# Small parameters on ScalarE's queue, input tiles turned first, and pick counts summed on TensorE, in a fused attention, state-space, convolution and mixture-of-experts layer

## The reference

```
h    = rms_norm(x, mix_norm);  proj = h @ w_in
c_q, c_kv, k_pe, u_ssm, conv_a, conv_g = split(proj)
y    = [rms(attention(c_q, c_kv, k_pe)), rms(s5(u_ssm)), rms(conv(conv_a, conv_g))]
x    = x + y @ w_out
h    = rms_norm(x, ffn_norm)
group     = argmax(h @ w_grp + b_grp)                 # 4 groups
two picks = top 2 of softmax((h @ w_exp + b_exp)[group])   # 8 experts in a group
x    = x + sum over the 2 picks: gate * ((silu(h @ w1[e]) * (h @ w3[e])) @ w2[e])
```

## Time and profile before

| | us |
|---|---|
| median of three runs | 1185.1 |
| the profiled execution | 1186.63 |
| its span, from first to last instruction | 1184.9 |
| TensorE busy | 1123.3 (95%) |
| VectorE busy | 977.1 (82%) |
| ScalarE busy | 704.5 (59%) |
| POOL busy | 372.2 (31%) |
| mean granted TensorE clock | 0.988 |

### The profile page before, as it was taken

One profiled execution on the slowest core, in us unless ns is written; L12 is line 12 of the kernel. 1 busy time (PEld: TensorE's weight loads), 2 busy tenths in 40 slices (PEclk: granted clock), 3 DMA queues, 4 the chain that ended last, 5 costly groups with the idle time before them and its releaser, 6 DMA issues.

```text
span 1184.9 us, 16010 instructions
## 1 busy us (share of the span) xinstructions
PE 1123.3 (95%) x5762; PEld 870.5 (73%) x5762; DVE 977.1 (82%) x1203; ACT 704.5 (59%) x825; POOL 372.2 (31%) x350
## 2 busy tenths in 40 slices
PE   6999999889999799998899999999999999999996
PEld 3457464766676577888788888888888888888885
DVE  5999989666666754367999999999999999999993
ACT  6521226655465541223577777777777777777772
POOL 4231012378971000112223323323323333333321
PEclk9999999999999999998999999999999999999998
DMA  8300010000006012236999999999999999999962
GB/s 294 95 1 1 1 25 5 1 1 2 1 2 249 1 37 83 84 127 235 387 369 373 374 397 379 390 400 386 393 379 391 391 367 372 395 378 369 388 236 55
DMA packets 40840, 260.96 MB, mean 220 GB/s; under 512 B 16366, under 2 KB 17114, under 8 KB 26970
## 3 DMA queue, kind: packets, MB, share of 16 engines
q1 hardware_dynamic: 30698, 243.03, 52.1%
q0 software_dynamic: 10096, 17.34, 6.0%
HBM read 252.26 MB, written 26.35 MB: 235 GB/s over the span
## 4 chain that ended last, share of the span: by engine, by line
PE 83%; DVE 9%; ACT 3%; issue 2%; DMA 1%; POOL 0%; POOLq 0%; SPq 0%; DVEq 0%; ACTq 0%
PE psum L2237 31%; PE psum L2257 15%; PE psum L1846 8%; PE psum L2145 7%; PE psum L2063 4%; PE psum L2093 3%; PE psum L1899 3%; DVE arena L1144 2%; PE psum L2227 2%; PE psum L2081 2%; PE psum L2243 1%; DVE am L1489 1%; DVE w_rest L1667 1%; PE psum L1949 1%; PE psum L2049 1%
## 5 line engine op out<-in xcount | busy, mean ns | idle before, releaser
L1667 DVE TENSOR_TENSOR w_rest<-w,w_high 128x2048 fp32r<-128x2048 f32 x136 | 305.2, 2286 | 18.7 <-ACT w_high L1056 17.0
L1056 ACT ACTIVATE w_high<-w 128x2048 fp32r<-128x2048 f32 x136 | 256.1, 1912 | 45.2 <-PE psum L2237 42.0
L2237 PE MATMUL psum<-w_high,xgT_high 128*128 128x512 f32 x544 | 216.2, 398 | 3.1 <-DVE xgT_rest L1712 3.1
L2237 PE MATMUL psum<-w_rest,xgT_high 128*128 128x512 f32 x544 | 213.4, 392 | 0.0
L2237 PE MATMUL psum<-w_high,xgT_rest 128*128 128x512 f32 x544 | 212.7, 391 | 0.0
L1719 DVE TENSOR_TENSOR w_rest<-w,w_high 128x2048 fp32r<-128x2048 f32 x66 | 148.0, 2283 | 0.0
L691 POOL DMA_INDIRECT out<-arena,idx x34 | 91.4, 2688 | 99.5 <-DVE arena L1732 94.2
L1066 ACT ACTIVATE w_high<-w 128x2048 fp32r<-128x2048 f32 x66 | 122.4, 1905 | 0.0
L2237 PEld LDWEIGHTS psum<-w_high,xgT_high 128*128 128x128 f32 x544 | 102.7, 189 | 23.7 <-issue 2.2
L2237 PEld LDWEIGHTS psum<-w_rest,xgT_high 128*128 128x128 f32 x544 | 102.5, 188 | 22.0
L2237 PEld LDWEIGHTS psum<-w_high,xgT_rest 128*128 128x128 f32 x544 | 102.8, 189 | 20.5
(11 more groups left out here) (303 smaller groups left out, 2049.2 us busy)
## 6 DMA issues: line engine op xcount, KB each, us to landing
w<-in_w SPq DMA_DIRECT2D x102, 2048.0 KB, 10.7
arena<-in_x SPq DMA_DIRECT2D x5, 1024.0 KB, 8.7
h_scratch<-arena SPq DMA_DIRECT2D x8, 512.0 KB, 2.7
out<-arena SPq DMA_DIRECT2D x8, 512.0 KB, 3.6
arena<-in_x SPq DMA_DIRECT2D x1, 3072.0 KB, 19.0
arena<-in_w_in SPq DMA_DIRECT2D x1, 2688.0 KB, 10.6
arena<-in_w_in SPq DMA_DIRECT2D x1, 2048.0 KB, 13.3
wout_y_raw<-in_w_out SPq DMA_DIRECT2D x1, 2048.0 KB, 7.8
```

Source lines behind the costliest of these rows:

```text
L1056: act.activation(w13h[k][:, c, :], w13[b][k][:, c, :], ACT.Copy).then_inc(W13H_READY[k], 1)
L1667: dve.tensor_tensor(w13l[b][k][:, c, :], w13[b][k][:, c, :], w13h[k][:, c, :].bitcast(F32), S_).then_inc(W13_SPLIT[k], 1)
L2237: last = pe.matmul(psum[:, k, :], x_[:, c, :], w_[:, c, :], start=(c == 0 and n == 0), stop=(c == KC - 1 and n == 2))
```

## The change

Head: the four small loads go from SP's queue to the start of ScalarE's, `log_dt` first; SP issues the first two pairs of x back to back. VectorE scales tiles 0 and 1 before it waits for the turned small rows. TensorE turns tiles 0 and 1 before it turns the small rows.

Routing: `prior` and its memset and eight additions are gone. VectorE makes one sum over the four tiles of part 0, `half_count`. TensorE adds the count of earlier tiles itself: for each tile i but the last of the part, `ones` times `both[:, i]`, broadcast to all later tiles of the part, and in part 1 `ones` times `half_count`, broadcast to all four. The totals are a function of their own, `counts`, five products into bank 7 behind `ranks(1)`. The filler ahead of `ranks(1)` goes from 28 to 16 transposes. In `place` the test for block 0 is folded into the two products that used it. The three operations on `nov` go from before the saving of the table to after the second split of expert 0's weights.

```diff
@@ SP
             load_x(0)
-            for k, lam in enumerate((lam_re, lam_im)):
-                sp.dma_start(first_rows[k * NPAIR:(k + 1) * NPAIR, :], ...).then_inc(first_rows_in, 16)
-            sp.dma_start(first_rows[2 * NPAIR:2 * NPAIR + KC, :], mix_norm[0]...).then_inc(first_rows_in, 16)
-            sp.dma_start(ldt..., log_dt[0].partition_broadcast(P)).then_inc(first_rows_in, 16)
             load_x(1)
@@ ScalarE, ahead of everything
+            act.dma_start(ldt..., log_dt[0].partition_broadcast(P)).then_inc(first_rows_in, 16)
+            act.dma_start(first_rows[2 * NPAIR:2 * NPAIR + KC, :], mix_norm[0]...).then_inc(first_rows_in, 16)
+            for k, lam in enumerate((lam_re, lam_im)):
+                act.dma_start(first_rows[k * NPAIR:(k + 1) * NPAIR, :], ...).then_inc(first_rows_in, 16)
@@ VectorE
+            scale_x(0)
+            scale_x(1)
             dve.wait_ge(hi_filled, R_P1 + 1)
             link(dve.tensor_copy(lamc...)); link(dve.tensor_copy(normc...))
-            scale_x(0)
             for h in range(2):
                 ts(v(0)..., ldt..., 1.0 / 16, None, M_)
             ts(v(1), v(0), 1.0 / 9, 1.0, M_, A_)
-            scale_x(1)
             exp_terms(8, 6)
@@ choose
                 tt(both[:, i0:i1], pick[0][:, i0:i1], pick[1][:, i0:i1], A_)
-                dve.sem_inc(picks_ready, 1)
                 if part == 0:
-                    link(dve.memset(prior[:, 0, :], 0.0))
-                for i in range(i0, i1):
-                    tt(prior[:, i + 1, :], prior[:, i, :], both[:, i, :], A_)
+                    link(dve.reduce_sum(half_count, both[:, i0:i1].rearrange("p t e -> p e t"), AX))
                 dve.sem_inc(picks_ready, 1)
@@ place
-                ts(f0, bk, 0.0, None, ALU.is_equal)
-                tt(vt, f0, tokf[:, i0:i1]..., M_)
-                tt(vg, f0, gate[:, :, i0:i1], M_)
+                stt(vt, order, P - 0.5, tokf[:, i0:i1]..., ALU.is_lt, M_)
+                stt(vg, order, P - 0.5, gate[:, :, i0:i1], ALU.is_lt, M_)
@@ VectorE behind place(1)
-            ts(nov, psum[:, 3, 0:NE], 63.5, 1.0 / P, A_, M_)
-            ts(nov, nov, ROUND, None, A_)
-            ts(nov, nov, ROUND + 1.0, 0.0, S_, ALU.max)
             dve.wait_ge(tab_filled, 2)
@@ VectorE behind rest_w13(1, 0, 0)
+            dve.wait_ge(counts_filled, 1)
+            ts(nov, psum[:, 7, 0:NE], 63.5, 1.0 / P, A_, M_)
+            ts(nov, nov, ROUND, None, A_)
+            ts(nov, nov, ROUND + 1.0, 0.0, S_, ALU.max)
@@ TensorE, head
+            turn_x(0, 2)
             pe.wait_ge(first_rows_in, 16 * 4)
             pe.transpose(psum[:, 5, 0:n], first_rows[:, :], ident[0:n, 0:n]).then_inc(hi_filled, 1)
@@ ranks
-                pe.matmul(o, before[:, :], both[:, i0:i1]..., start=True, stop=False)
-                pe.wait_ge(picks_ready, 2 * part + 2)
-                last = pe.matmul(o, ones[:, :], prior[:, i0:i1]..., start=False, stop=True)
+                pe.matmul(o, before[:, :], both[:, i0:i1], start=True, stop=False, ...)
                 if part == 1:
-                    last = pe.matmul(psum[:, 3, 0:NE], ones[:, :], prior[:, NT, :], start=True, stop=True)
+                    pe.matmul(o, ones[:, :], half_count.unsqueeze(1).to_broadcast([P, i1 - i0, NE]), ...)
+                for i in range(i0, i1 - 1):
+                    last = pe.matmul(o[:, i + 1 - i0:, :], ones[:, :], both[:, i, :].unsqueeze(1).to_broadcast([P, i1 - 1 - i, NE]), ...)
+            def counts():
+                pe.matmul(psum[:, 7, 0:NE], ones[:, :], half_count, start=True, stop=False)
+                for i in range(*ROUTE[1]):
+                    last = pe.matmul(psum[:, 7, 0:NE], ones[:, :], both[:, i, :], start=False, stop=(i == NT - 1))
+                last.then_inc(counts_filled, 1)
@@ TensorE, around part 1
-            keep_busy(psum[:, 0, :], 28)
+            keep_busy(psum[:, 0, :], 16)
             ranks(1)
+            counts()
             keep_busy(psum[:, 0, :], 28)
             table(1)
```

More of the change, by code:

```diff
@@ L203, in build @@
         both = at(R0 + 1408, NT, NE)
-        prior = at(R0 + 1664, NT + 1, NE)
+        half_count = at(R0 + 1664, NE)
         nov, novend, one32 = (at(R0 + 1952 + NE * k, NE) for k in range(3))
@@ L763, in _ @@
         def _(act):
+            with nc.allow_non_contiguous_dma(reason="parameters of a few KiB"):
+                act.dma_start(ldt.rearrange("p r h -> p (r h)"), log_dt[0].partition_broadcast(P)).then_inc(first_rows_in, 16)
+            act.dma_start(first_rows[2 * NPAIR:2 * NPAIR + KC, :], mix_norm[0].rearrange("(c p) -> c p", p=P)).then_inc(first_rows_in, 16)
+            for k, lam in enumerate((lam_re, lam_im)):
+                act.dma_start(first_rows[k * NPAIR:(k + 1) * NPAIR, :], lam[0].rearrange("(r h) s -> r (h s)", h=2)).then_inc(first_rows_in, 16)
             seq = [0]
@@ L1627, in place @@
                 pk, wk = picks[:, :, i0:i1], work[:, :, i0:i1]
-                order, bk, rw, f0 = (v_[:, :, i0:i1] for v_ in (order_, nth, row, first))
+                order, bk, rw = (v_[:, :, i0:i1] for v_ in (order_, nth, row))
                 vt, vg = val[:, 0, :, i0:i1], val[:, 1, :, i0:i1]
@@ L1637, in place @@
                 stt(rw, bk, -float(P), order, M_, A_)
-                ts(f0, bk, 0.0, None, ALU.is_equal)
-                tt(vt, f0, tokf[:, i0:i1].unsqueeze(1).to_broadcast([P, 2, n_t]), M_)
-                tt(vg, f0, gate[:, :, i0:i1], M_)
+                stt(vt, order, P - 0.5, tokf[:, i0:i1].unsqueeze(1).to_broadcast([P, 2, n_t]), ALU.is_lt, M_)
+                stt(vg, order, P - 0.5, gate[:, :, i0:i1], ALU.is_lt, M_)
                 for n in range(2):
@@ L1848, in project, with turn_x @@
                 last.then_inc(lo_filled, 1)
-            def turn_x(half):
-                for i in range(4 * half, 4 * half + 4):
+            def turn_x(i0, i1):
+                for i in range(i0, i1):
                     pe.wait_ge(x_normed, i + 1)
@@ L1873, in _ @@
             for half in range(2):
-                turn_x(half)
+                turn_x(4 * half + (0, 2)[half == 0], 4 * half + 4)
                 if half == 1:
@@ L2175, in ranks @@
                 i0, i1 = ROUTE[part]
-                pe.wait_ge(picks_ready, 2 * part + 1)
-                o = psum[:, RANK_BANK[part], 0:(i1 - i0) * NE]
-                pe.matmul(o, before[:, :], both[:, i0:i1].rearrange("p t e -> p (t e)"), start=True, stop=False)
-                pe.wait_ge(picks_ready, 2 * part + 2)
-                last = pe.matmul(o, ones[:, :], prior[:, i0:i1].rearrange("p t e -> p (t e)"), start=False, stop=True)
-                if part == 1:
-                    last = pe.matmul(psum[:, 3, 0:NE], ones[:, :], prior[:, NT, :], start=True, stop=True)
-                last.then_inc(ranks_filled, 1)
+                pe.wait_ge(picks_ready, part + 1)
+                o = psum[:, RANK_BANK[part], 0:(i1 - i0) * NE].rearrange("p (t e) -> p t e", e=NE)
+                pe.matmul(o, before[:, :], both[:, i0:i1], start=True, stop=False, skip_group_check=True)
+                if part == 1:
+                    pe.matmul(o, ones[:, :], half_count.unsqueeze(1).to_broadcast([P, i1 - i0, NE]), start=False, stop=False,
+                              skip_group_check=True)
+                for i in range(i0, i1 - 1):
+                    last = pe.matmul(o[:, i + 1 - i0:, :], ones[:, :], both[:, i, :].unsqueeze(1).to_broadcast([P, i1 - 1 - i, NE]),
+                                     start=False, stop=(i == i1 - 2), skip_group_check=True)
+                last.then_inc(ranks_filled, 1)
+            def counts():
[3 more added lines that the diff above has]
+                last.then_inc(counts_filled, 1)
             def table(part):
```

1 line of the change is left out of this document (added).

## The result

The changed kernel takes 1189.2 us (median of 10 runs, 1188.14 to 1191.7), the kernel before 1185.13 (median of 10 beside it, 1184.11 to 1187.79). The ratio is 1.0029, 95% interval 1.0019 to 1.004: about 3.4 us slower. Forecast were 1185.1 and, with 16 in 100, a slower kernel. The forecast is wrong, and 1189.2 lies above its range of 1182.2 to 1188.0.

The account below looks back on a forecast made before the run. TensorE was taken as the bound (83% of the span), VectorE in the routing. Head +1.1, first half -0.77, second half -1.0, counts +0.65 summed to 0.0: 1185.1 us median, 1186.6 profiled, range 1182.2 to 1188.0.

Parts of the forecast that it names:

- the late first pair: Head: small loads beside the first pair of tiles were costed as delaying it 0 us, other end 0.7 us.
- rival B: Head: clock still low when the projection starts, each product 0.88 us instead of 0.44; 1.95 us more, 1187.1; chance 0.12.
- the second half of the routing: Routing: picks ready sooner and fewer fillers let VectorE place earlier; gain 1.0 us, ends 0.6 and 1.7.
- the order: Head: tiles 0 and 1 first delays VectorE's series and idles TensorE; projection 1.1 us later, at 19.4, ends +0.3 and +1.8.
- Routing, first half: Routing: VectorE swaps a memset and four additions for one sum; gate work starts 0.77 us sooner, all gain.
- Rival A: Routing: clock stays low past the second ranks, so fillers hold up the table; sum +2.8 us, 1187.9; chance 0.12.
- The counts: Routing: three operations on the counts, moved behind expert 0's second split, make TensorE wait for VectorE; cost 0.65 us.
- C: Second expert's products: the low clock stretch at 581.6 us goes, worth 1.7 us; with head's lower end -2.5, 1182.6; chance 0.18.
- D: Head: second pair lands no sooner, at 11.39, making no difference, 1185.1; chance 0.58 together with the forecast.
- E: Head: small rows on the new queue land late, after 11.85; held excluded up to 2.8 us, no chance given.

## Why the prediction was wrong

Four terms of the sum missed. In the traces the change's own terms come to +6.2 us where the sum had 0.0: the late first pair, put at 0, +2.05; the clock in the projection, left out of the sum as rival B, +2.19; the second half of the routing +0.37 in place of -1.0; the order +1.60 in place of +1.1. The runs show a loss of 3.4 us, and show it in the head alone. Between 6.2 and 3.4 lie stretches of low clock that a single execution has or lacks, such as the one at 195 us; how much they make in the median no run here settles.

**The first pair: the failed step.** "I cost their delay of the first pair at 0; the other end is 0.7 us." The delay was 1.8 us (5.63 to 7.44), outside both ends. I judged it by the engines' free share in 1 to 2 us, and took the hole at 5 to 6 us as time that the new queue would win back for the second pair. It did (that pair was there by 9.90, before at 11.39), but the broadcast now runs while the first pair does, and there it costs more than the end I gave it. The prediction named the consequence, that every step slips with it, but gave it no chance of its own.

The Trainium skill (DMA: Bandwidth & Descriptors, "Issuing engines are not separate DMA queues") says that loads from other engines share the same 16 engines and interleave, so that only time to issue is saved. I used it to bound the gain. The runs show that the same rule holds a price as well: here 1.8 us for the first pair, which the broadcast had not touched as long as it stood behind that pair in the same queue.

**Rival B came true on top.** "In the head the clock is still low when the projection starts", chance 0.12, priced at +1.95: measured 2.19. (What the prediction calls a product there is an entry, half a product; the price is the same.) My argument against it, 3.3 us of transposes right ahead, doesn't hold: they stood ahead of it in the changed kernel and in three more with the new order (9.30; 9.50, 9.32 and 8.74 for the 16 entries). In the kernel with the three short loads on ScalarE's queue the 16 entries took 7.11. Windows of that kernel and of the one with log_dt alone there (columns as in the earlier trace rows):
```profile
15.70:16.10 0.40, 0.39 (x3) 0.39 (x4) 0.33 (x3) 0.00 (x0) 0.00 (x0) 0.99 1.01 430
16.20:19.40 3.20, 2.96 (x14) 2.33 (x12) 2.96 (x11) 1.99 (x4) 0.00 (x0) 0.50 1.00 396
```
```profile
18.40:25.00 6.60, 5.79 (x15) 3.32 (x15) 6.12 (x24) 5.33 (x9) 1.91 (x4) 0.50 0.75 128
```
In both the clock was up when the transposes of tile 2 began, behind 3.2 us of idle time, and fell within them. In the one it was back before the projection, in the other 3.3 us into it. In the changed kernel these transposes were slow from the first. So B came in four of the five profiles with the new order and an unfilled gap, and what decides it between two executions is open.

**The order was right in its mechanism.** With the pair in time and the clock back, the order cost 1.59 us at the row behind the first 16 entries; forecast were 1.1 for the start, with an end at 1.8. Of the 0.5 by which its start missed (19.90 against 19.4), 0.36 is that TensorE turned the small rows at 12.21 and not at 11.85: between its last transpose and them lie 0.33 us that the prediction left out. VectorE waited for no rms, as forecast. The sum in the trace: 1.60 order + 2.05 late pair and what follows it (19.90 to 21.95 in the start: 1.82 for the pair, 0.23 because all sixteen transposes of tiles 2 and 3 ran at the lower level, 3.68 against 3.45) + 2.19 clock in the projection = 5.84. Timed, the two edits of the head cost 0.3% (3.6 us, interval 1.9 to 5.2).

**Routing, first half**: forecast 0.77, measured 0.69. Right.

**Routing, second half: wrong by its clock.** "I expect it still low" was said of the ranks only; for the logits and the first table I kept the 1.98 us of before. In all but two profiles of the new routing the clock had fallen by then; the half gave back 0.37 in place of gaining 1.0. With the clock up it gains 0.9 to 1.5; forecast were 1.0, with 1.7 as the end. Rival A didn't come: the clock was back before the second fillers, which took 3.25. What I feared there, fillers that end after the rows are ready, didn't decide either.

**The counts**: forecast 0.65, measured 0.65.

**C**, the low stretch at 581.6 gone, didn't come: after 2.16 us idle the granted clock over 586.1 to 590.0 was 0.56 again:
```profile
586.10:590.00 3.90, 3.85 (x10) 3.09 (x11) 3.62 (x7) 1.30 (x1) 0.00 (x0) 0.56 1.01 429
```
**D** is refuted (the second pair came sooner), **E** as excluded (the small rows waited for TensorE, not for their loads).

So in the traces: head +5.84, the low stretch at 195 us absent -1.65, first half -0.69, second half +0.37, counts +0.65: +4.52 at the second expert's first product (581.63 to 586.15), and 4.9 at the end of the span. What lies in the last 0.4 I have not traced.

**Left open.** Why the clock falls ahead of the last logits in six of eight profiles of the new routing and in none of six of the old. Filling the idle time ahead of them kept it up in the one profile there is, but the head with its gap filled kept it up too, without. And the 2.1 us of that profile (66.35 to 64.24) were not found in time: the interval of 0.998 to 1.0012 allows them at its edge, the medians show none. No version here is shown to beat the kernel before.

## What to carry to other kernels

Before a small load is moved to another queue, ask which large load it then runs beside, and who waits for that one first; a broadcast with a packet for each partition is not small by its bytes. Where an order is changed, look at what TensorE did in the microseconds ahead of its bulk work: a gap put there is paid in transposes and can be paid again in the first products. And cut work out of a chain only together with the question what the clock will be in it: here the same edit lost 0.4 us or won 0.9 to 1.5 by that alone.

## What the runs showed of the hardware

- The load of log_dt, a row of 16 values (64 bytes) broadcast to 128 partitions, on a second queue, made the 1 MB load ahead of it 1.8 us late (first square at 7.38 to 7.54 in five profiles, 5.57 to 5.79 in nine) and held the rate in 4 to 5 us at 206 GB/s against 410. With log_dt alone the queue carried 144 packets and 0.01 MB. The Trainium skill (DMA: Bandwidth & Descriptors, "Queues, rings and completion order") says that each DMA engine takes turns between queue rows packet by packet; that would let the broadcast's packets in between those of the pair, where in one queue they stand behind. The delay agrees, the turns themselves no run here shows.
- The record of the granted clock can say 1.00 in the head where the pace says half. From 22 to 26.3 us in the kernel after, with entries 0.86 us apart:
```profile
22.00:26.30 4.30, 4.30 (x5) 1.77 (x6) 3.80 (x19) 4.26 (x8) 1.73 (x4) 1.00 0.87 192
```
In two other kernels it did show 0.50 in the head (16.2 to 19.4 and 18.4 to 25.0 us, shown above), where the pace agrees. So a 1.00 in the head has to be checked by the distance of like instructions.
- Being busy throughout did not bring the clock back soon: from 542 to 551 us in the kernel after TensorE had no idle time, in logits, table and transposes, and the granted clock stayed at 0.50.
